# Fillers between SBUF tiles that move every matmul operand to a multiple of 128 bytes

## What is computed

```python
xl = _layernorm(x + pos, ...);  xc = _layernorm(ctx, ...)
hl = modulate(xl)                         # adaLN shift and scale from silu(c)
pl = split(hl @ w_in + b_in)              # 1024 x 5120: u, q, v, f_fwd, f_bwd, og, gates
mix = g_four * (fourier_mix(u) @ w_fp) + g_hgrn * (hgrn(q, v, f, og) @ w_hp)
xl = _layernorm(ALPHA * xl + mod[2] * (mix @ w_o + b_o), ...)
xl = _layernorm(ALPHA * xl + mod[5] * (square(relu(h2 @ w1 + b1)) @ w2 + b2), ...)   # h2 = modulate(xl)
```

## The kernel before

| tiles | before | with the change |
|---|---|---|
| `all_ident`, `all_mean` | 0 | 0 |
| `head_cTh`, `cTl`, `wh`, `wl`, `x` | 96 | 0 |
| `head_hTh0` to `hTl3`, `early`, `silb`, `wa`, `rows` | 32 | 0 |
| `mix_kq`, `kx`, `ks`, `qr`, `v`, `kdT`, `pm`, `st`, `stb`, `qd` | 96 | 0 |
| `mix_m2`, `m3`, `fa`, `fx` | 32 | 0 |
| all of `merge_` | 96 | 0 |
| all placed tiles of `tail_` | 96 | 0 |

## Time and profile before

### The profile page before, as it was taken

One profiled execution on the slowest core, in us unless ns is written; L12 is line 12 of the kernel. 1 busy time (PEld: TensorE's weight loads), 2 busy tenths in 40 slices (PEclk: granted clock), 3 DMA queues, 4 the chain that ended last, 5 costly groups with the idle time before them and its releaser, 6 DMA issues. The chain is left out here.

```text
span 3383.8 us, 35637 instructions
## 1 busy us (share of the span) xinstructions
PE 3140.5 (93%) x14552; PEld 2562.5 (76%) x14552; DVE 1852.5 (55%) x2585; ACT 615.2 (18%) x1048; POOL 301.3 (9%) x453
## 2 busy tenths in 40 slices
PE   5999999999996899929969999999999999999997
PEld 3878788888884688826758878888888778888886
DVE  3831133121222888657758775666655666666556
ACT  1421000111112556521001221111111101111110
POOL 0323011000001212200000000000000000000000
PEclk8999999999998999969989999999999999999999
DMA  6642233233235533345554721221114321111111
GB/s 216 208 138 78 75 101 124 103 122 115 96 107 165 150 109 111 99 158 193 173 172 148 226 77 48 63 69 63 56 48 126 122 69 58 58 60 60 50 44 62
DMA packets 261127, 365.32 MB, mean 108 GB/s; under 512 B 15443, under 2 KB 171363, under 8 KB 259430
## 3 DMA queue, kind: packets, MB, share of 16 engines
q1 hardware_dynamic: 203926, 197.33, 19.2%
q0 software_dynamic: 43680, 134.26, 11.4%
q10 hardware_dynamic: 13360, 31.46, 2.9%
HBM read 256.55 MB, written 106.44 MB: 107 GB/s over the span
## 5 line engine op out<-in xcount | busy, mean ns | idle before, releaser
L137 PE MATMUL head_bank<-head_hTh,head_wh 128*128 128x512 f32 x1024 | 407.2, 398 | 3.1 <-DVE head_hTl L549 2.3
L1971 PE MATMUL tail_bank<-tail_h2h,tail_w1h 128*128 128x512 f32 x1024 | 400.8, 391 | 4.5 <-DVE tail_w1l L1740 4.5
L139 PE MATMUL head_bank<-head_hTh,head_wl 128*128 128x512 f32 x1024 | 404.9, 395 | 0.0
L138 PE MATMUL head_bank<-head_hTl,head_wh 128*128 128x512 f32 x1024 | 404.9, 395 | 0.0
L1989 PE MATMUL tail_bank<-tail_w2h,tail_ah 128*128 128x512 f32 x1024 | 400.2, 391 | 4.0 <-DVE tail_acc L1770 4.0
L1972 PE MATMUL tail_bank<-tail_h2l,tail_w1h 128*128 128x512 f32 x1024 | 400.4, 391 | 0.0
L1973 PE MATMUL tail_bank<-tail_h2h,tail_w1l 128*128 128x512 f32 x1024 | 400.1, 391 | 0.0
L1990 PE MATMUL tail_bank<-tail_w2l,tail_ah 128*128 128x512 f32 x1024 | 399.8, 390 | 0.0
L1991 PE MATMUL tail_bank<-tail_w2h,tail_al 128*128 128x512 f32 x1024 | 399.8, 390 | 0.0
L557 DVE CAST head_wh<-head_raw 128x1024 fp32r<-128x1024 f32 x64 | 44.5, 695 | 583.5 <-PE head_bank L139 432.0
L1772 DVE TENSOR_TENSOR tail_acc<-tail_acc,tail_bank 128x512 f32<-128x512 f32 x416 | 275.6, 684 | 118.5 <-PE tail_bank L1991 116.4
(11 more groups left out here) (228 smaller groups left out, 4755.8 us busy)
## 6 DMA issues: line engine op xcount, KB each, us to landing
tail_raw<-in_w SPq DMA_DIRECT2D x128, 512.0 KB, 4.0
head_raw<-in_w_in SPq DMA_DIRECT2D x64, 512.0 KB, 4.1
scratch_proj<-head_stage POOLq DMA_DIRECT2D x128, 256.0 KB, 2.7
head_x<-in_w_ada ACTq DMA_DIRECT2D x8, 2048.0 KB, 10.1
merge_gates<-scratch_proj SPq DMA_DIRECT2D x32, 512.0 KB, 5.1
head_wa<-in_w_ada SPq DMA_DIRECT2D x8, 1024.0 KB, 5.3
mix_dec<-scratch_proj SPq DMA_DIRECT2D x32, 256.0 KB, 3.9
scratch_dft_a<-mix_fa POOLq DMA_DIRECT2D x32, 256.0 KB, 4.0
```

The source lines that it names most:

```text
L137: nc.tensor.matmul(out, wh, xh, start=(k == 0), stop=False)
L138: nc.tensor.matmul(out, wh, xl, start=False, stop=False)
L139: last = nc.tensor.matmul(out, wl, xh, start=False, stop=(k == k_tiles - 1))
L1971: nc.tensor.matmul(U[2 * e + c][:], w1h[:, e, k, :], hT[0][:, k, cs], start=(k == 0), stop=False)
```

## The change

Before each group of tiles that matmuls read, `bx.line(name)` opens a filler tile that is as long as the distance to the next multiple of 128 bytes, if that is not 0. `mod2` and `mod5` are opened behind such a filler and so come after the small tiles, as before. The fillers are 32 bytes in `build_program`, 64 bytes before `hT` in `phase_in` and 64 before `m2` in `phase_mix`; the one in `phase_tail` comes out empty. Nothing writes or reads a filler. Each engine has the same instructions in the same order with the same semaphores as before; only addresses in them differ. Small tiles behind the moved ones (statistics, `tail_b1`, `tail_xr`) shift by 32 bytes as well.

```diff
@@ constants
+LINE = 128
@@ class Box
+    def line(self, name):
+
+        gap = -(-(-self.nc.sbuf_base // 32) * 32) % LINE
+        if gap:
+            self.sb(f"line_{name}", [P, gap // 4])
@@ phase_in
         std, rstd = bx.sb("std", [P, 2]), bx.sb("rstd", [P, 2])
+        bx.line("hT")
         base = -(-nc.sbuf_base // 32) * 32
         hT = [(bx.sb(f"hTh{c}", [P, KD, 512], F32R), bx.sb(f"hTl{c}", [P, KD, 512], F32R)) for c in range(NC)]
@@ phase_mix
         tot = bx.sb("tot", [P, NU, 2, H])
+        bx.line("m2")
         m2 = bx.sb("m2", [P, 2, 2 * P])
@@ phase_tail
     with Box(nc, "tail") as bx:
+        bx.line("tail")
         base = -(-nc.sbuf_base // 32) * 32
@@ build_program
             "b_in_col": bx.sb("b_in_col", [P, 40]),
-            "mod2": bx.sb("mod2", [P, D]),
-            "mod5": bx.sb("mod5", [P, D]),
             "primed": 0,
             "settled": bx.sem("settled"),
         }
+        bx.line("mods")
+        for name in ("mod2", "mod5"):
+            g[name] = bx.sb(name, [P, D])
```

## The result

The forecast was 145.5 us less; the change brought 23.5 us. Against the 3242.7 us of the prediction stands a median of 3365.4 us. That lies inside the stated range of 3232 to 3370 us, but only because the range was drawn out to the first rival; the forecast itself, and the mechanism behind its largest terms, did not come true.

A forecast was written before the change was run, and what follows sets the result against it. Between the seams the prediction took TensorE's matmul pitch to bound the kernel; 65.7 + 15.0 + 53.8 + 10.4 + 2.0 - 1.4 = 145.5 us off 3388.2 gave 3242.7 us, range 3232 to 3370 us.

The forecast's parts named there:

- the first rival: Equal offsets alone count: MLP stays at 226.7 ns, strips and pairs fall to it; 22.5 us, 3366 us; chance 0.24.
- the price at offset 0: All 512-column fp32r matmuls: pitch with both operands at offset 0, bounded by 216.0 and 226.7 ns, taken as 216.0.
- the MLP's 65.7 us: MLP products: 6 x 1024 matmuls fall from 226.7 to 216.0 ns, saving 65.7 us.
- 15.0 of merge and output projection: Merge and output projection: 2 x 768 matmuls save 10.7 ns each, 16.4 us, of which 15.0 us is seen.
- 2.0 of the context tokens: Input projection's strips on context tokens, 256 columns: 192 matmuls fall from 120 to 109.3 ns, saving 2.0 us.
- strips and pairs: Input projection: latent-token strips fall from 233.5 to 216.0 ns, 53.8 us; pairs (u and v rows) from 228.7, 10.4 us.
- the pieces: Moving operand fetched in 128-byte pieces: 2048 bytes off alignment touch 17 instead of 16, making 544 cycles; offset 0 removes this.
- a second loss: Input projection's strips: 48 surplus cycles, not 32, taken to come where the two operands lie at different offsets.
- 1.4 us would have been given back: Last down product of each MLP half: VectorE thinly covered, 0.11 us lost on some 6 tiles each, 1.4 us.
- the other 1.4 us: First 36 merge and 96 output projection matmuls end ahead of a weight wait VectorE splits; 1.4 us of gain unseen.
- Nothing changes: Whole kernel: granule is 32 bytes or less and every tile already begins on one; 3388 us; chance 0.08.
- Slower, by collisions at one and the same place: All at offset 0: moving stream, weight load and VectorE collide, 6.8 ns on 6144 + 1536 matmuls; 3440 us; chance 0.08.

The follow-up runs named there:

- probe3: No kernel change: 31 streams of 48 matmuls with varied distances, steps and types; fp32r with moving step 0 218.3 ns, bf16 with every second element 225.7 ns.
- probe1: No kernel change: 37 matmul streams with varied offsets (0 to 96 bytes), widths and types; fp32r at 512 columns 226.8 ns at equal offsets 0, 32, 64, 96.

## Why the prediction was wrong, point by point

**What failed: the price at offset 0.** The part on the change had bounded a matmul with both operands at 0 by 216.0 and 226.7 ns and took the lower end, "since both lengths in cycles fit the piece of 128 bytes exactly and since half clock removes the surplus whole". The upper end was the true one, and with it go the MLP's 65.7 us, 15.0 of merge and output projection, 2.0 of the context tokens, and 10.7 ns each of what strips and pairs were to bring. Measured at 0 are 226.6 ns in the MLP and the output projection, 226.7 in the merge and 120 on the context tokens. Both reasons were facts, and neither tells the pieces from a fixed surplus. 32 cycles at 256 and at 512 columns are the same 32 cycles for one piece more as for a fixed start-up of the stream. Half clock only says that the loss lies beside the array, which holds for both. (That the surplus is no plain constant either, the 113.4 ns of 256 columns at (0, 64) and the 48 cycles at 448 columns show.) And no row of before had an fp32r matmul at 0, so the fit rested on the one thing that was not in the trace. What argued against it was in the trace too: by the pieces, a moving operand at 32 touches 17 of them just as one at 96, so they say nothing of the 6.8 ns between strips and MLP. The prediction saw that ("it does not explain") and gave it to "a second loss", which was the only one that an address could change.

**What held.**
- The second loss comes with unequal offsets and goes with them, at 512 columns: 3072 x (233.4 - 226.8) ns = 20 us of strips and 816 x (228.7 - 226.6) ns = 2 us of pairs, of 23.0 us by the spans. Only its condition was too loose, 128 for 256 bytes.
- The surplus goes with the moving stream's fetch; the witness is probe3. The reading of the earlier trace rows hardly shows it, since 0.49 us in steps of 0.01 us cannot tell 13.5 ns well, and probe3 also shows that the weight load is not without effect.
- Plain f32 and half clock show next to nothing of it, and both stayed.
- VectorE and ScalarE took the same time with their tiles moved to 0: 1851.5 and 616.3 us busy for 1852.5 and 615.2.
- Nothing came late behind the faster matmuls, since they did not become faster in the MLP; whether 1.4 us would have been given back there was not put to the test. Nor was the other 1.4 us, taken off the merge and the output projection; for the latter name the split of the activations, `tail_ys`, as the releaser, and not that of the weights.

**The other rivals.** "Nothing changes" is refuted by the ratio. "Slower, by collisions at one and the same place": the MLP's pitch at (0, 0) is 226.6 ns, and in probe1 (0, 0) equals (96, 96). Equal places are the good case, not the bad one.

**What stays open.** Why the stream needs 32 cycles more and not another number, and why the surplus is 48 and 40 at 448 and 480 columns; why a distance that is no multiple of 256 adds up to 8 ns at 512 columns, with 192 cheaper than the rest, and takes up to 7 ns off at 256 columns; why equal offsets of 16 and 4 bytes are dear. Moving stream and weight load meeting in some part of the memory would fit some of this; no run shows it.

## What to carry to other kernels

When two fp32r operands of one 512-column matmul stream at full rate, compare their addresses with each other, modulo 256 bytes, before aligning each by itself: equal at any multiple of 32 is as good as aligned, and aligned but 128 apart is as bad as 64 apart. Do not carry this to other widths unmeasured: at 256 columns every unequal pair tried was at least as fast as the equal one. A surplus that shows in one number of cycles for all cases seen may be a fixed price; before a forecast rests on removing it, look for one case in the trace that lacks it, and where there is none, give the end without a gain the larger chance. A stream of 48 equal matmuls for each candidate, one source line each, settles such a question in one run.

## What the runs showed of the hardware that was not expected

- The pitch of an fp32r 128x512 matmul with both operands at multiples of 32 bytes depends on (stationary - moving) modulo 256 bytes: 226.8 ns at 0, 229 at 192, 232.6 to 234.4 elsewhere; bf16 and plain f32 streams show no such dependence at the offsets tried. At 256 columns it is the other way: 120 ns at 0, 113.4 at 64.
- Both operands at 16 have 230.2 ns, at 4 238.1 ns.
- A matmul stream that passes over 4 bytes a column at full clock has 226 to 227 ns for 512 columns at distance 0 whatever its type (fp32r, or bf16 with step 2); one that passes over 2 has 215.7.
- A narrower stationary tile at (0, 0) makes the stream slower, not faster: (11.22 - 0.39) / 47 = 230.4 ns at 64 columns, for 226.8 at 128.
- So does a stationary tile with a step: 233.4 ns with every second element, 235.1 with every fourth.
